# The state-space stage's three GpSimd products moved to VectorE in a three-layer transformer kernel

## The reference

```python
def ssd_mixer(z, xbc, dt, conv_w, conv_b, dt_bias, a_log, d_skip, norm_g):
    xbc = jax.nn.silu(causal_conv(xbc, conv_w, conv_b))
    ...                                        # split into xs, bm (B), cm (C)
    dtc = jax.nn.softplus(dt + dt_bias)
    a_cum = jnp.cumsum(dtc * a, axis=2)        # a = -exp(a_log)
    lmat = jnp.exp(jnp.where(tril, seg, -jnp.inf))
    cb = jnp.einsum('bcign,bcjgn->bcijg', cm, bm)
    y_diag = jnp.einsum('bcijg,bcijgh,bcjgh,bcjghp->bcighp', cb, lmat, dtc, xs)
    decay_states = jnp.exp(a_cum[:, :, -1:] - a_cum)
    states = jnp.einsum('bcjgn,bcjgh,bcjghp->bcghpn', bm, decay_states * dtc, xs)
    ...                                        # scan of states over the 4 chunks: h_in
    y_off = jnp.einsum('bcign,bcghpn,bcigh->bcighp', cm, h_in, jnp.exp(a_cum))
    y = y_diag + y_off + xs * d_skip
    y = rms_norm_2(y * jax.nn.silu(z), norm_g)
```

## Time and profile before

| | |
|---|---|
| Median of 3 runs | 3234.25 us (3234.22 to 3234.89) |
| Profiled execution, whole | 3237.18 us |
| Its span | 3235.4 us |
| TensorE busy | 2928.4 us, 91% |
| VectorE busy | 1633.1 us, 50% |
| ScalarE busy | 1118.9 us, 35% |
| GpSimd busy | 114.6 us, 4% |
| Mean granted TensorE clock | 0.933 |

### The profile page before, as it was taken

One profiled execution on the slowest core, in us unless ns is written; L12 is line 12 of the kernel. 1 busy time (PEld: TensorE's weight loads), 2 busy tenths in 40 slices (PEclk: granted clock), 3 DMA queues, 4 the chain that ended last, 5 costly groups with the idle time before them and its releaser, 6 DMA issues.

```text
span 3235.4 us, 38406 instructions
## 1 busy us (share of the span) xinstructions
PE 2928.4 (91%) x13615; PEld 2310.6 (71%) x13615; DVE 1633.1 (50%) x2963; ACT 1118.9 (35%) x1836; POOL 114.6 (4%) x108
## 2 busy tenths in 40 slices
PE   7699999988998999998778996889899968999998
PEld 4354788876887788886656886558677746778887
DVE  1221744544555472634873215773677765355362
ACT  1332322224553332223353221872254433232221
POOL 0000000000000000000000000000122210000000
PEclk9799999988998999998889975999899988999999
DMA  3101232311111132231101230002211101323221
GB/s 114 36 33 46 92 109 91 101 62 53 52 58 46 52 111 97 94 100 66 52 1 52 93 109 1 1 1 92 72 65 59 63 22 66 117 92 103 91 100 69
DMA packets 60648, 221.32 MB, mean 68 GB/s; under 512 B 6512, under 2 KB 6640, under 8 KB 60400
## 3 DMA queue, kind: packets, MB, share of 16 engines
q1 hardware_dynamic: 58928, 213.43, 20.0%
q0 software_dynamic: 1600, 6.29, 0.5%
HBM read 215.50 MB, written 4.19 MB: 68 GB/s over the span
## 4 chain that ended last, share of the span: by engine, by line
PE 73%; DVE 13%; issue 6%; ACT 4%; DVEq 4%; ACTq 0%; DMA 0%; POOL 0%; SPq 0%; POOLq 0%
PE ps L332 19%; PE ps L334 19%; PE ps L333 19%; PE ps L316 3%; PE ps L429 2%; PE ps L421 2%; DVE work L1671 1%; DVEq L2537 1%; DVE big L2481 1%; DVE work L1690 1%; PE ps L1189 1%; PE ps L2031 1%; DVE sq L889 1%; PE ps L2011 1%; DVE ring_lo L282 1%
## 5 line engine op out<-in xcount | busy, mean ns | idle before, releaser
L332 PE MATMUL ps<-a_hi,ring_hi 128*128 128x512 f32 x1776 | 720.2, 405 | 39.7 <-DVE ring_lo L282 17.1
L282 DVE TENSOR_TENSOR ring_lo<-ring,ring_hi 128x1024 fp32r<-128x1024 f32 x366 | 447.9, 1225 | 580.4 <-ACT ring_hi L275 546.8
L333 PE MATMUL ps<-a_lo,ring_hi 128*128 128x512 f32 x1776 | 699.9, 394 | 0.0
L334 PE MATMUL ps<-a_hi,ring_lo 128*128 128x512 f32 x1776 | 699.9, 394 | 0.0
L275 ACT ACTIVATE ring_hi<-ring 128x1024 fp32r<-128x1024 f32 x366 | 384.7, 1055 | 528.1 <-PE ps L334 525.5
L332 PEld LDWEIGHTS ps<-a_hi,ring_hi 128*128 128x128 f32 x1776 | 339.1, 191 | 124.0 <-issue 20.7
L333 PEld LDWEIGHTS ps<-a_lo,ring_hi 128*128 128x128 f32 x1776 | 339.9, 191 | 73.8 <-issue 6.0
L334 PEld LDWEIGHTS ps<-a_hi,ring_lo 128*128 128x128 f32 x1776 | 338.8, 191 | 72.8
L332 PE MATMUL ps<-hid_hi,ring_hi 128*128 128x512 f32 x896 | 351.0, 392 | 11.1 <-DVEq L923 11.1
L334 PE MATMUL ps<-hid_hi,ring_lo 128*128 128x512 f32 x896 | 350.3, 391 | 0.0
L333 PE MATMUL ps<-hid_lo,ring_hi 128*128 128x512 f32 x832 | 324.6, 390 | 0.0
(11 more groups left out here) (361 smaller groups left out, 3742.0 us busy)
## 6 DMA issues: line engine op xcount, KB each, us to landing
ring<-weights SPq DMA_DIRECT2D x399, 512.0 KB, 3.5
h<-x SPq DMA_DIRECT2D x1, 2048.0 KB, 8.4
residual<-h POOLq DMA_DIRECT2D x2, 1024.0 KB, 4.8
h<-residual POOLq DMA_DIRECT2D x1, 2048.0 KB, 10.9
out<-h POOLq DMA_DIRECT2D x1, 2048.0 KB, 7.6
tab<-tables SPq DMA_DIRECT2D x1, 1648.0 KB, 12.1
big<-positions SPq DMA_DIRECT2D x1, 256.0 KB, 13.7
col<-columns SPq DMA_DIRECT2D x1, 164.5 KB, 9.1
```

The costliest lines, as they stand in the source:

```text
L282: dve.tensor_tensor(lo, M.ring[:, b % RING, :], hi.bitcast(F32), ALU.subtract).then_inc(M.sem("blocks_split"), 1)
L332: pe.matmul(out, w_hi, hi, start=start, stop=False)
L333: pe.matmul(out, w_hi, lo, start=False, stop=False)
L334: return pe.matmul(out, w_lo, hi, start=False, stop=stop)
```

## The change

All three products of GpSimd in this stage are done by VectorE, and GpSimd has no instruction left in it.

- Product A (L2639) becomes `gate_x(g, s)`. It stands one step late: the product of tile s - 1 comes after the `rest_block` of step s, and that of tile 5 ahead of the gate of step 6. It ends with a drain.
- Product B (L2651) stands behind the four dt weightings and a drain, ahead of the masking of CB. The semaphore `ssd_xdt` is gone.
- Product C (L2655) stands directly ahead of the head's `decay` product and waits, as that does, for both exponentials.

```diff
@@ -2484,12 +2484,23 @@
             dve.nop().then_inc(M.sem("ssd_conv"), 1)
             dve.nop().then_inc(M.sem("ssd_free"), 1)
             rest_block(dve, M, FIRST["ssd_in"] + n + 2)
+            if s:
+                gate_x(g, s - 1)
         else:
+            if s == 6:
+                gate_x(g, 5)
             dve.wait_ge(M.sem("ssd_sig"), n)
             dve.tensor_tensor(R.gate[g % 2][s - 6], M.bank(n % 2), R.sig[n % 2], ALU.mult)
             dve.drain().then_inc(M.sem("ssd_gate"), 1)
             dve.nop().then_inc(M.sem("ssd_free"), 1)
             rest_block(dve, M, FIRST["ssd_in"] + n + 2)
+
+    def gate_x(g, s):
+        n = STEPS * g + s + 1
+        dve.wait_ge(M.sem("ssd_sig"), n)
+        x = R.conv[g % 2][s]
+        dve.tensor_tensor(x, x, R.sig[n % 2], ALU.mult)
+        dve.drain().then_inc(M.sem("ssd_x"), 1)
 
     heads = lambda x: x.rearrange("p (h d) -> p h d", d=64)
 
@@ -2511,8 +2522,16 @@
         if s == 0:
             for c in range(QT):
                 dve.wait_ge(M.sem("ssd_x_turned"), QT * g + c + 1)
-                dve.tensor_tensor(heads(R.x_tok[c]), heads(M.bank(3 + c)), by_head(R.dtc, c, g), ALU.mult)\
-                   .then_inc(M.sem("ssd_xdt"), 1)
+                dve.tensor_tensor(heads(R.x_tok[c]), heads(M.bank(3 + c)), by_head(R.dtc, c, g), ALU.mult)
+            dve.drain()
+            if g:
+
+                dve.wait_ge(M.sem("ssd_out_mm"), HPG * g)
+            else:
+                dve.wait_ge(M.sem("ssd_to_end"), 1)
+            for c in range(N_STATE):
+                dve.tensor_tensor(heads(R.xw[c]), heads(R.x_tok[c]), by_head(R.to_end, c, g), ALU.mult)\
+                   .then_inc(M.sem("ssd_xw"), 1)
             dve.wait_ge(M.sem("ssd_cb"), g + 1)
             four = lambda x: x.rearrange("p (c i) -> p c i", c=QT)
             dve.tensor_tensor(four(R.cb), four(M.bank(7)), M.t("tri", P).unsqueeze(1).broadcast_to([P, QT, P]),
@@ -2522,6 +2541,7 @@
             e = s - 2
             h = 8 * g + e
             dve.wait_ge(M.sem("ssd_decay"), h + 1)
+            dve.tensor_tensor(R.c_dec[e % 2], R.c_dec[e % 2], R.conv[g % 2][5], ALU.mult).then_inc(M.sem("ssd_c_dec"), 1)
             dve.tensor_tensor(R.decay[e % 2], R.decay[e % 2], R.cb, ALU.mult).then_inc(M.sem("ssd_decay_cb"), 1)
         if 1 <= s <= 8:
             e = s - 1
@@ -2625,48 +2645,6 @@
                        lambda k: M.hid_lo[:, k, :], lambda k: M.hid_hi[:, k, :])
 
     branch_out_dve(dve, M, "ssd_out", 2, 4, scale, last=True)
-
-
-def ssd_pool(pool, M, R):
-    heads = lambda x: x.rearrange("p (h d) -> p h d", d=64)
-
-    def project(g, s):
-
-        if s < 6:
-            n = STEPS * g + s + 1
-            pool.wait_ge(M.sem("ssd_sig"), n)
-            x = R.conv[g % 2][s]
-            pool.tensor_tensor(x, x, R.sig[n % 2], ALU.mult).then_inc(M.sem("ssd_x"), 1)
-
-    def mix(g, s):
-        if s == 0:
-            if g:
-
-                pool.wait_ge(M.sem("ssd_out_mm"), HPG * g)
-            for c in range(N_STATE):
-                pool.wait_ge(M.sem("ssd_xdt"), QT * g + c + 1)
-                if g == 0 and c == 0:
-                    pool.wait_ge(M.sem("ssd_to_end"), 1)
-                w = R.to_end[:, c, 8 * g:8 * g + 8].unsqueeze(2).broadcast_to([P, 8, 64])
-                pool.tensor_tensor(heads(R.xw[c]), heads(R.x_tok[c]), w, ALU.mult).then_inc(M.sem("ssd_xw"), 1)
-        if 1 <= s <= 8:
-            e = s - 1
-            pool.wait_ge(M.sem("ssd_exp_c"), 8 * g + e + 1)
-            pool.tensor_tensor(R.c_dec[e % 2], R.c_dec[e % 2], R.conv[g % 2][5], ALU.mult)\
-                .then_inc(M.sem("ssd_c_dec"), 1)
-
-    for s in range(STEPS):
-        project(0, s)
-    for g in range(GRPS):
-        for s in range(STEPS):
-            if s != 1:
-                mix(g, s)
-            if g + 1 < GRPS:
-                project(g + 1, s)
-            if s == 1:
-                mix(g, s)
-
-
 
 
 def to_h_dve(dve, M, name, per_tile, unroll, banks, looped=True, ahead=None, base=0, given=False):
@@ -2775,7 +2753,6 @@
             dsa_pool(pool, M, dsa)
             pool.wait_ge(M.sem("nsa_cmp_kept"), 4)
             pairs_pool(pool, M, nsa.pairs, "nsa_norm", 11)
-            ssd_pool(pool, M, ssd)
 
             pool.wait_ge(M.sem("blocks_used"), FIRST["mix_out"] - 2)
             pool.dma_start(M.h[:, :, :], residual.rearrange("(k p) t -> p k t", p=P))\
```

## The result

The changed kernel takes 3245.49 us in the median of 8 runs (3241.46 to 3246.27), the kernel before 3234.92 in 8 runs beside it (3232.40 to 3235.61): ratio 1.0032, 95% interval 1.0022 to 1.0043. It is slower by 7 to 14 us. The profiled executions are 3246.27 us against 3237.18, their spans 3244.1 against 3235.4.

What follows compares the result with a forecast made beforehand. TensorE was taken to bound full groups except where it waits, a VectorE and ScalarE chain the last group. Full groups 5.0 us plus last group 3.2 make 8.2, 3242.4 us on the median of 3234.25; range 3236 to 3250.

Steps and rivals of the forecast that it cites:

- GpSimd's products held VectorE's: State-space stage: VectorE's two-input products stand still until GpSimd's product ends; without these they return to 0.69 us.
- five decay products held for 1.11 us: Full group: five VectorE decay products each give back 1.11 us, part of 9.3 us back against 11.5 us arriving.
- The sum of the path: VectorE's queue in a full group, followed to head 7: 2.53 us late, 0.87 covered, 1.66 not.
- Prices of 0.60 and 0.81: VectorE's queue: each moved product costs 0.60 us without a drain, 0.81 us with one.
- Full groups, 1.66 us each: Each of the three full groups gets longer by the uncovered 1.66 us at head 7, 5.0 us in all.
- It was idle for 3.71 us there: VectorE's idle time at the end of a full group's first projection, taken to hide the three state weightings' 2.0 us.
- Last group, 3.2 us: Last group, no projection beside it: 1.76 us before the first state plus 4.80 for heads, minus 3.32 returned.
- First stretch, 0: Projections and convolutions before the first full group: no delay reaches TensorE, 0 us, with 0.5 us as other end.
- Sum: Whole kernel: 5.0 us from full groups plus 3.2 us from the last group, 8.2 us slower.
- Faster: Rival, full groups: returned stalls outweigh the moved products, at best some 3225.5 us; chance 0.07.
- Hidden slack in the ring: Rival, full groups: the wait loop over ScalarE has slack, so they cost 0 to 0.6 us; 3237 to 3239 us; chance 0.17.
- The clock: Rival, full groups: TensorE's clock falls at the turn, 2 to 3 us more per group, 3248 to 3252 us; chance 0.13.

Runs made afterwards that it cites:

- late_on_gpsimd: Kernel before with only GpSimd's queue reordered: product A of step s - 1 comes behind product C of step s, nothing moved to VectorE; 3231.54 us, ratio 0.9990.
- extra_on_gpsimd: The whole change plus 18 GpSimd products that nobody reads, each started by a convolution tile's sigmoid; ratio 1.0067 against the kernel before.
- no_drain: The whole change, but product A signals by itself and not through a drain behind it; ratio 1.0024 against the kernel before.
- b_only: Kernel before with product B alone moved to VectorE, A and C staying on GpSimd; ratio 1.0010.
- c_behind: The whole change, but product C stands behind the next head's differences in steps 6 to 9 and in the last group; ratio 1.0049 against the kernel before.
- a_only: Kernel before with product A alone moved to VectorE, one step late with its drain, B and C staying on GpSimd; ratio 0.9999.
- c_only: Kernel before with product C alone moved to VectorE, ahead of the head's decay product, A and B staying on GpSimd; ratio 1.0030.

## Why the prediction was right, step by step

- **GpSimd's products held VectorE's: right.** Shown from both sides: the rows fall to 0.69 us when GpSimd's work goes (the change) or only moves in time (late_on_gpsimd), and rise to 1.53 when unneeded work is put there (extra_on_gpsimd). The Trainium skill's rule (SBUF — State Buffer, Who interferes with whom), that the second to issue waits out the whole of the first, agrees but for 0.14 us: by it the product of 2478.06 would end at 2479.73. One reading beside it was wrong: the prediction counts five decay products held for 1.11 us in a full group, and the rows have four (heads 1 to 4). So 8.2 us come back against 11.5, not 9.3. The sum of the path used four, and stands.
- **Prices of 0.60 and 0.81: right**, 0.60 and 0.80 in the rows after, and no_drain took out the difference of 0.2 five times a group.
- **Full groups, 1.66 us each: 2.03, 1.87 and 2.15.** The mechanism was right, step by step. In the first full group, counted from the turn, the decay products of heads 3, 4 and 7 end at 52.07, 59.98 and 85.30 us where before had 51.34, 58.94 and 82.45: later by 0.73, 1.04 and 2.85, forecast 0.43, 0.73 and 2.53 and, as below, 0.25 that the first group adds. What isn't covered is seen as the wait of 1.04 us before head 7. Two small terms were missing. "It was idle for 3.71 us there" was read in the second group. In the first group VectorE was idle for only 1.81 us there, and the three weightings reach past its idle time, as the timeline of the change has it:

```profile
2349.34 2.48 DVE L2525 TENSOR_TENSOR work<-ps,work 128x512 f32<-128x512 f32 x4
2351.90 1.90 DVE L2533 TENSOR_TENSOR work<-work 128x512 f32<-128x512 f32 x3
2353.71 0.69 DVE L2537 TENSOR_TENSOR work<-ps,tab 128x512 f32<-128x512 f32 x1
2354.48 0.81 DVE L2478 TENSOR_SCALAR big<-ps,col 128x512 f32<-128x512 f32 x1
```

The convolution starts 9.02 us after the turn (2345.46) where before it started 8.77 after it; b_only, which has B alone, is 0.23 us longer in that group. The others are VectorE's idle times on issue, 0.7 us in group 2 (0.5 of before to take off) and 0.6 in group 3. With them the sums are 1.91, 1.9 and 2.3, together 6.1 where 6.05 was measured. Why VectorE has more of them than before stays open; they stand at the same steps with the same lengths in the full groups of c_behind and extra_on_gpsimd, so they come with the program and not with one execution.
- **Last group, 3.2 us: 3.57.** TensorE's timeline, and in the last row VectorE's:

```profile
2617.69 2.81 PE L2313 MATMUL ps<-work 128*128 128x512 f32 x6 [2.12 <-DVE work L2533]
2623.34 3.26 PE L2325 MATMUL ps<-work,tab 128*128 128x512 f32 x4 [2.85 <-DVEq L2519]
2630.49 0.92 PE L2339 MATMUL ps<-work 128*64 128x128 f32 x4 [3.89 <-DVE work L2545]
...
2668.73 0.65 PE L2339 MATMUL ps<-work 128*64 128x128 f32 x4 [0.84 <-DVE work L2545]
...
2672.50 1.50 DVE L2567 TENSOR_TENSOR ssum<-ssum,sq 128x512 f32<-128x512 f32 x2 [0.47 <-issue]
```

Head 0 comes 2.7 us later than before where 1.76 + 0.60 was forecast: the two cumulated decays ran at half the clock (3.26 us for 1.98 in before, granted clock 0.5 from 2623.91 to 2627.32), after a wait of 2.85, and VectorE's first differences start 1.59 us behind their beginning where it was 1.17. From head 0 to head 7 another 0.5 us is lost where 0.9 was forecast. The sum had not counted that in two steps of before the differences came 0.82 us behind the decay product's start and not 0.60 (2626.22 to 2627.04, 2642.91 to 2643.73). So head 7 is 3.22 us later after the turn, just the forecast, and that is in part luck: two misses of 0.4 cancel. The last 0.35 us came behind it, with an idle time of 0.47 on issue before the last sum of squares (2672.50).
- **First stretch, 0: right.** From the first convolution (L2478, 2295.00 us, before 2295.10) to the first turn (2345.46, before 2345.51) it is 50.46 us, before 50.41.
- **Sum.** 8.2 forecast, 9.6 in the stage, 9.1 between the profiled executions, 10.6 between the medians. Only the stage's own number can be followed term by term: executions of one kernel lie up to 10 us apart (3227.35 to 3237.17 for the kernel before in 26).
- **Rivals.** Faster would have needed products of 0.55 us. Hidden slack in the ring is refuted by the 8.44 us from differences to differences, 0.6 more than the 7.84 of before (2499.36 to 2507.20). The clock did not fall in the full groups (1.00), in spite of the new wait; it fell in the last group (0.78, before 0.85), for some tenths of a microsecond.

What the sum did not show is how uneven the parts are. Alone, A costs nothing, B 2.8 us and C 9.8 us, together 12.5 where the change is 9.6. In the three full groups the parts nearly add up: A -1.1, B +0.3, C +7.2, together 6.4, and the change has 6.05; A's removal from GpSimd pays for part of C. Nearly all of the difference is in the last group (A +1.0, B +2.6, C +2.5, together 6.15 against 3.57), and 2.3 of its 2.6 us lie behind the start of head 7: a_only and c_only lose 1.4 and 1.2 us there, at half the clock, the change only 0.35, at the full one.

## What to carry to other kernels

When a VectorE product with two inputs in SBUF takes 0.9 to 1.1 us more than the same product elsewhere, look at GpSimd's timeline in the same microseconds before changing anything: here reordering GpSimd's queue, so that its products ran beside instructions that it doesn't hold, gave the stalls back for nothing (1.1 us a group), while moving the work gave them back for 0.6 to 0.8 us per product. Cost a moved product by its place in the queue and in a ring of waits. The gated products alone were free because stalls of the same size went with them, not because the queue had room: the 0.2 us of their drains counted in full. The 0.60 us ahead of each head counted nearly in full as well. And before turning the order of two instructions round, follow every engine that the later one releases; the leg over TensorE cost 4 to 7 us where only the one over ScalarE had been counted.

## What the runs showed of the hardware that I had not expected

- The hold works in both directions. GpSimd's A took 1.82 us beside VectorE's L282, and 1.27 to 1.30 where it ran beside the convolution's multiply-adds alone (three of six in the second full group of late_on_gpsimd; the other three, 1.72, began beside a product of VectorE).
- The stage's first convolution (L2478) begins at 2289.96 to 2295.10 us in ten profiles of kernels that are alike up to there, and from it to the first turn it is 50.39 to 50.56 us in all of them. So executions differ by up to 5 us before it. A difference of 3 us is better read from the stage's own span.
- TensorE's clock in the last group depends on small shifts: four matmuls of head 7 took 0.65 us in before, in b_only and in the change, and 1.05, 0.83 and 0.82 in a_only, c_only and no_drain, where the granted clock fell to 0.5 within 0.4 us of their start. From head 7 to L421 that is worth 1.2 to 1.4 us.
